# One step of a hybrid decoder on one core: ScalarE weighs the value pages of odd units, VectorE adds them, TensorE keeps those of even units

## What is computed

```
z = q . k / sqrt(128) + bias[h]                    # 8 heads
log_keep = log_sigmoid(-z);  after = sum of log_keep over later keys
a = exp(log_sigmoid(z) + after)
out[h, :] = sum over keys of a[key, h] * v[key, h, :]
```

## Time and profile before

| | us |
|---|---|
| median of 3 runs | 2443.89 |
| lowest, highest run | 2442.11, 2444.17 |
| profiled execution, device time | 2445.29 |
| profiled execution, span | 2443.6 |
| TensorE busy | 2409.5 |
| VectorE busy | 1749.0 |
| ScalarE busy | 1137.6 |
| GpSimd busy | 377.9 |

### The profile page before, as it was taken

How to read it: one execution, slowest core, us unless ns; L and a number is a source line. 1 busy time by engine, 2 the same in 40 slices (tenths; PEclk the granted TensorE clock), 3 DMA queues, 4 the chain that set the end, 5 groups by cost and what they waited for, 6 DMA issues and landing times.

```text
span 2443.6 us, 47247 instructions
## 1 busy us (share of the span) xinstructions
PE 2409.5 (99%) x19728; PEld 2386.2 (98%) x19728; DVE 1749.0 (72%) x2190; ACT 1137.6 (47%) x1719; POOL 377.9 (15%) x375
## 2 busy tenths in 40 slices
PE   8999999999999989999999999999999999999999
PEld 8999999999999989999999999999999999999999
DVE  6379767566665478888888888787888888877333
ACT  6343223334553365555555555555555555555221
POOL 0011111111101320112121212121212121213000
PEclk9999999999999999999999999999999999999999
DMA  6255666464342442566665656565656565685323
GB/s 216 95 193 207 246 238 216 155 211 140 127 173 96 144 161 96 148 147 150 146 153 144 154 144 154 144 155 143 153 144 154 147 150 148 150 190 222 117 87 105
DMA packets 135590, 382.60 MB, mean 157 GB/s; under 512 B 14026, under 2 KB 58186, under 8 KB 126674
## 3 DMA queue, kind: packets, MB, share of 16 engines
q1 hardware_dynamic: 72450, 285.16, 33.9%
q0 software_dynamic: 62640, 94.28, 20.2%
q10 hardware_dynamic: 288, 0.14, 0.0%
HBM read 309.18 MB, written 73.55 MB: 157 GB/s over the span
## 4 chain that ended last, share of the span: by engine, by line
PE 84%; DVE 9%; ACT 2%; issue 2%; DMA 1%; POOL 0%; SPq 0%; ACTq 0%; DVEq 0%; POOLq 0%
PE out_ps L2029 24%; PE tok_mix L2275 15%; PE pair_ps L2275 12%; PE out_ps L2259 9%; PE out_ps L2275 8%; PE out_ps L2348 5%; PE out_ps L2152 3%; PE pair_ps L2348 3%; DVE w_lo L1729 2%; DVE w_sum L1741 2%; PE tok_mix L2348 1%; PE pair_ps L2068 1%; ACT w_hi L1208 1%; DVE w_lo L1734 1%; DMA w_raw<-w_units 1%
## 5 line engine op out<-in xcount | busy, mean ns | idle before, releaser
L2029 PE MATMUL out_ps<-x_hi,w_hi 128*128 128x260 f32 x1792 | 379.1, 293 | 12.1 <-DVE w_lo L1581 7.8
L1208 ACT ACTIVATE w_hi<-w_sum 128x1024 fp32r<-128x1024 f32 (+1 forms) x252 | 215.4, 855 | 341.6 <-DVE w_sum L1741 246.4
L2029 PE MATMUL out_ps<-x_hi,w_lo 128*128 128x260 f32 x1792 | 362.2, 284 | 0.0
L2029 PE MATMUL out_ps<-x_lo,w_hi 128*128 128x260 f32 x1792 | 361.8, 284 | 0.0
L1729 DVE TENSOR_TENSOR w_lo<-w_sum,w_hi 128x1024 fp32r<-128x1024 f32 (+1 forms) x252 | 244.7, 971 | 134.4 <-ACT w_hi L1208 133.8
L1208 ACT ACTIVATE w_hi<-w_raw 128x1024 fp32r<-128x1024 f32 (+1 forms) x306 | 261.2, 865 | 135.5 <-PE out_ps L2259 102.4
L2275 PE MATMUL tok_mix<-op_hi,w_hi 128*128 128x260 f32 x1056 | 297.1, 281 | 1.5 <-ACT part L1250 1.5
L2275 PE MATMUL tok_mix<-op_hi,w_lo 128*128 128x260 f32 x1056 | 298.1, 282 | 0.0
L2275 PE MATMUL tok_mix<-op_lo,w_hi 128*128 128x260 f32 x1056 | 297.5, 282 | 0.0
L2029 PEld LDWEIGHTS out_ps<-x_hi,w_hi 128*128 128x128 f32 x1792 | 279.8, 190 | 15.2 <-DVE w_lo L1581 7.8
L906 POOL DMA_DIRECT2D h_dram<-staging x110 | 146.7, 1485 | 926.5 <-DVE staging L1890 909.2
(11 more groups left out here) (305 smaller groups left out, 6105.9 us busy)
## 6 DMA issues: line engine op xcount, KB each, us to landing
w_raw<-w_units SPq DMA_DIRECT2D x239, 512.0 KB, 4.0
w_raw<-w_units SPq DMA_DIRECT2D x57, 1024.0 KB, 5.4
w_fifth<-w_units SPq DMA_DIRECT2D x58, 512.0 KB, 3.9
h_dram<-staging POOLq DMA_DIRECT2D x110, 260.0 KB, 6.8
k_ring<-cache_k SPq DMA_DIRECT2D x50, 512.0 KB, 5.0
v_ring<-cache_v POOLq DMA_DIRECT2D x38, 512.0 KB, 4.9
h_dram<-part POOLq DMA_DIRECT2D x50, 260.0 KB, 6.7
q_dram<-staging POOLq DMA_DIRECT2D x40, 260.0 KB, 6.4
```

Source lines behind the costliest of these rows:

```text
L1208: act.activation(dst, src, ACT.Copy).then_inc(hi_done, 1)
L2029: mm = pe.matmul(out_ps[:, 2 * (t % 2) + a, 0:HALF], w[:, u % 2, cols], x[:, a * HALF:(a + 1) * HALF], start=first and n == 0, stop=last a ...
```

## The change

A table of pages (`V_PLAN`) says for each by whom it is weighed, in which unit, when it is added and in which slot it lies. Samples 0 to 2 stay with TensorE. From unit 25 to 39 each odd unit has two pages that ScalarE weighs and VectorE adds at the unit's end; even units 26 to 34 have two on TensorE; 36, 38 and 40 have two, two and one that VectorE weighs and adds; unit 41 has one on TensorE. Sample 7 stays with ScalarE, now wholly in places of `o_cm`, weighed in units 41 to 45. In all TensorE has 35 pages in place of 48, ScalarE 24 in place of 8, VectorE 5 in place of 8; it adds 24 times in place of 14, and there are 5 totals in place of 2 (units 28, 32, 36, 41, 45). The total of a sample is the slot of its first page not on TensorE. GpSimd's due times are set anew. The squares of the samples' columns are made in one piece (64 columns) and halved three times, and the last head's squares now count as the first of two steps of `sb_sum_done`; SyncE's wait for one step stays as it is written, TensorE waits for two. `h` tiles 6 to 11 are loaded in unit 41 of SyncE's list.

```diff
@@ -222,53 +222,92 @@
-V_FIRST = [16, 19, 22, 25, 28, 31]
-BY_TENSOR = len(V_FIRST)
-N_TENSOR = BY_TENSOR * PAGES
...
-WEIGH_UNIT = dict(zip(range(SIXTH, N_PAGES), (35, 35, 36, 36, 37, 37, 38, 38) + (39, 39, 41, 41, 42, 43, 43, 44)))
-ADD_UNIT = dict(zip(range(SIXTH, N_PAGES), (35, 35, 36, 36, 37, 37, 38, 38) + (40, 40, 42, 42, 43, 44, 44, 45)))
-V_REDUCE = {39: BY_TENSOR, 45: BY_TENSOR + 1}
-V_SLOT = [j % V_SLOTS for j in range(SIXTH + 1)] + [1 + n % 2 for n in range(PAGES - 1)] + [2, 1, 4, 5, 6, 4, 5, 6]
...
+def v_plan():
+
+    odd = "scalar"
+    plan = [Page("tensor", 16 + 3 * b + pg // 3, None, (PAGES * b + pg) % V_SLOTS) for b in range(3) for pg in range(PAGES)]
+
+    def add(by, slots, weigh, added=None):
+        for slot, u, a in zip(slots, weigh, added or weigh):
+            plan.append(Page(by, u, None if by == "tensor" else a, slot))
+
+    for first, near, far in ((25, 1, 2), (29, 2, 1)):
+        add(odd, (0, near), (first, first))
+        add("tensor", (far, near), (first + 1, first + 1))
+        add(odd, (far, near), (first + 2, first + 2))
+        add("tensor", (far, near), (first + 3, first + 3))
+    add(odd, (0, 1), (33, 33))
+    add("tensor", (2, 1), (34, 34))
+    add(odd, (2, 1), (35, 35))
+    add("vector", (2, 1), (36, 36))
+    add(odd, (2, 1), (37, 37))
+    add("vector", (0, 1), (38, 38))
+    add(odd, (0, 1), (39, 39))
+    add("vector", (0,), (40,))
+    add("tensor", (1,), (41,))
+    add("scalar", (3, 4, 5, 6, 4, 5, 6, 4), (41, 41, 41, 42, 43, 43, 44, 45), (41, 42, 42, 43, 44, 44, 45, 45))
+    return plan
+
+
+V_PLAN = v_plan()
+V_SUM = {28: 3, 32: 4, 36: 5, 41: 6, 45: 7}
+V_UNITS = sorted({(page.weigh, j // PAGES) for j, page in enumerate(V_PLAN) if page.by == "tensor"} | set(V_SUM.items()))
...
+def v_freed(i):
+
+    page = V_PLAN[i]
+    if page.by == "tensor":
+        return page.weigh + (0.9 if i == v_pages(page.weigh)[-1] else 0.7)
+    if is_first(i):
+        return [u for u, b in V_SUM.items() if b == i // PAGES][0] + 0.6
+    late = i + 1 == len(V_PLAN) or V_PLAN[i + 1].add != page.add
+    return page.add + (0.85 if page.add % 2 and page.add < U_OUT else 0.5) + (0.08 if late else 0)
...
@@ -721,11 +757,10 @@
 
                     sp.wait_ge(z_s_done, SAMPLES)
                     sp.dma_start(h[:, 0:H_KEYS, :], x_t[:, 0:H_KEYS, :]).then_inc(h_in[0], 16)
-                if u == U_OUT:
-
-                    sp.wait_ge(v_used, N_TENSOR)
-                    sp.wait_ge(total_used, 1)
-                    sp.wait_ge(v_added, added(SEVENTH + 1))
+                if u == V_UNITS[-2][0]:
+
+                    sp.wait_ge(v_used, pages_by("tensor", N_PAGES - 1))
+                    sp.wait_ge(total_used, len(V_SUM) - 1)
                     sp.dma_start(h[:, H_KEYS:H_PAGES, :], x_t[:, H_KEYS:H_PAGES, :]).then_inc(h_in[1], 16)
                 if u == U_OUT + 4:
@@ -830,18 +865,21 @@
 
             def load_v(j):
                 page = pool.value_load(table[0:1, j:j + 1], min_val=0, max_val=N_PHYS - 1)
-                before = v_before(j)
-                if before is None and V_SLOT[j] >= V_SLOTS:
-                    pool.wait_ge(x_lo_done, KT + HEADS)
-                elif before is not None and before < N_TENSOR:
-                    pool.wait_ge(v_used, before + 1)
-                elif before is not None:
-                    pool.wait_ge(v_added, added(before))
-                elif V_SLOT[j] == RING:
-                    pool.wait_ge(q_rows_out, 16)
+                before, slot_of_v = v_before(j), V_PLAN[j].slot
+                if before is None:
+                    if slot_of_v >= V_SLOTS:
+                        pool.wait_ge(x_lo_done, KT + HEADS)
+                    elif slot_of_v == RING:
+                        pool.wait_ge(q_rows_out, 16)
+                elif V_PLAN[before].by == "tensor":
+                    pool.wait_ge(v_used, pages_by("tensor", before))
+                elif is_first(before):
+                    pool.wait_ge(total_used, sums_before(before // PAGES))
+                else:
+                    pool.wait_ge(v_added, adds_before(before))
                 pool.dma_start(v_slot(j),
                                cache_v[bass.ds(page, 1), :, :].rearrange("a p n -> (a p) n"))\
-                    .then_inc(v_in[V_SLOT[j]], 16)
+                    .then_inc(v_in[V_PLAN[j].slot], 16)
 
             def add_squares(x, total, cols, done=pool_step):
                 chained(pool.tensor_tensor(pool_sq[:, cols], x, x, ALU.mult))
-            freed = [U_OUT - 0.3 if v_before(j) is None else v_freed(v_before(j)) for j in range(V_SLOTS, N_PAGES)]
-            jobs = [(freed[j - V_SLOTS] + 0.8, "load", j) for j in range(V_SLOTS, N_PAGES)]
+            jobs = [(U_OUT + 0.45 if v_before(j) is None else v_freed(v_before(j)), "load", j)
+                    for j in range(V_SLOTS, N_PAGES)]
             jobs += [(U_MLP + 3.5 + 2 * i, "mlp", i) for i in range(HEADS)]
@@ -871,11 +909,16 @@
                     add_squares(o_cm[:, i, :], cm_r, slice(0, TOK), cm_sum_done if i == HEADS - 1 else pool_step)
                 else:
                     pool.wait_ge(tok_read, reads_before("av", U_KV + 3 + 2 * i) + 1)
-                    add_squares(q[:, i, 0:PROMPT], sb_r, slice(0, PROMPT))
+                    add_squares(q[:, i, 0:PROMPT], sb_r, slice(0, PROMPT),
+                                sb_sum_done if i == HEADS - 1 else pool_step)
             pool.wait_ge(v_read, len(V_UNITS))
-            for i in range(HEADS):
-                add_squares(q[:, i, PROMPT:TOK], sb_r, slice(PROMPT, TOK),
-                            sb_sum_done if i == HEADS - 1 else pool_step)
+            samples = q[:, :, PROMPT:TOK]
+            n = HEADS * SAMPLES
+            chained(pool.tensor_tensor(y[:, 0, 0:n].rearrange("p (h s) -> p h s", s=SAMPLES), samples, samples, ALU.mult))
+            while n > SAMPLES:
+                n //= 2
+                chained(pool.tensor_tensor(y[:, 0, 0:n], y[:, 0, 0:n], y[:, 0, n:2 * n], ALU.add))
+            pool.tensor_tensor(sb_r[:, PROMPT:TOK], sb_r[:, PROMPT:TOK], y[:, 0, 0:n], ALU.add).then_inc(sb_sum_done, 1)
...
@@ -1128,13 +1167,15 @@
                     act.wait_ge(out_read, t + 1)
                     square_head(2 * HEADS + i, y[:, t % 2, :])
                     if i:
+                        weigh_pages(u, 0)
                         act.wait_ge(arg_done, i)
                         act.activation(z[:, :], z[:, :], ACT.Exp).then_inc(a_done, 1)
                         weights_of_sample(u)
                     rstd(2 * HEADS + i)
                     if not i:
                         weights_of_sample(u)
-                    weigh_pages(u)
+                        weigh_pages(u, 0)
+                    weigh_pages(u, 1)
                     if i:
                         take_attention(i - 1)
                 elif u <= U_OUT:
...
 
             def add_page(j):
 
-                b, pg = divmod(j, PAGES)
-                if b > BY_TENSOR:
-                    dve.wait_ge(v_scaled, pg + 1)
-                if j == SEVENTH + 1:
-                    dve.wait_ge(x_lo_done, KT + HEADS)
-                total = v_place(V_TOTAL[b])
-                chained(dve.tensor_tensor(total, v_slot(j - 1) if pg == 1 else total, v_slot(j), ALU.add), v_added)
+                if V_PLAN[j].by == "scalar":
+                    dve.wait_ge(v_scaled, pages_by("scalar", j))
+                total = v_slot(v_first(j // PAGES))
+                chained(dve.tensor_tensor(total, total, v_slot(j), ALU.add), v_added)
 
             def pages_of(u):
 
...
 
-                pe.wait_ge(v_added, added(PAGES * b + PAGES - 1))
-                pe.wait_ge(v_read, V_UNITS.index((u, b)))
-                total = v_place(V_TOTAL[b])
+                first = v_first(b)
+                pe.wait_ge(v_added, adds_before(PAGES * (b + 1) - 1))
+                pe.wait_ge(v_read, V_UNITS.index((u, b)) - 1)
                 for hd in range(HEADS):
-                    mm = pe.matmul(o_s_ps(u, b)[:, hd:hd + 1], total[:, hd * P:(hd + 1) * P], ones[:, 0:1],
+                    mm = pe.matmul(o_s_ps(u, b)[:, hd:hd + 1], v_slot(first)[:, hd * P:(hd + 1) * P], ones[:, 0:1],
                                    start=False, stop=True, skip_group_check=True)
-                    between[2] = lambda: sum_features(sb_r, sb_sum_done, 1, (root_done, 3))\
+                    between[2] = lambda: sum_features(sb_r, sb_sum_done, 2, (root_done, 3))\
                         .then_inc(x_sum_ready, 1)
 
                 for at, j in zip((14, 11, 7), reversed(v_pages(u))):
                     between[at] = lambda j=j, u=u: weigh_values(j, u)
-                if u in V_REDUCE:
-                    between[14] = lambda u=u: sum_total(u, V_REDUCE[u])
+                if u in V_SUM:
+                    between[(14, 12, 7)[len(v_pages(u))]] = lambda u=u: sum_total(u, V_SUM[u])
```

More of the change, by code:

```diff
@@ L237 @@
[L237 to L242 removed]
+Page = namedtuple("Page", "by weigh add slot")
+def v_plan():
```

(13 more changed lines are left out.)

66 lines of the change are left out of this document (26 added, 40 removed).

## The result

| | before | after |
|---|---|---|
| median, us | 2444.03 | 2419.64 |
| lowest, highest run (4 runs each) | 2442.11, 2444.60 | 2419.37, 2419.89 |
| profiled execution: device time, span | 2445.29, 2443.6 | 2419.68, 2418.0 |

The ratio is 0.9897, 95% interval 0.9884 to 0.9910: 24.4 us less by the medians, 25.6 us by the two profiled executions. Predicted were 2418.0 us and, against the profiled execution, 25.9 us.

What follows compares the result with a forecast made beforehand. TensorE, busy 2409.5 of 2443.6 us, was taken as the bound. Gains of 17.8 + 2.0 + 6.1 = 25.9 us took 2445.29 to 2419.4, less 1.4 to the median: 2418.0 us, range 2415.0 to 2427.0.

Steps and rivals of the forecast that it cites:

- The sum of the pages, 17.8 us: TensorE, units 25 to 47: 13 pages less, three totals more, net 10 page prices of 1.78 us.
- The 23.8 us of unit 29: Unit 29's length before the change, 460.40 to 484.18; without its three pages of 1.78 us, 18.5 us.
- ScalarE at price 0: Odd units 25 to 39: two pages weighed, 4.9 us a unit, fit into ScalarE's idle times; nothing on the path.
- VectorE at price 0: 8.5 us more VectorE work; an odd unit's two adds fit where it idled 9.94 us; nothing on the path.
- GpSimd's order, 2.0 us: Page loads issued before attention squares; unit 38's pages arrive on time, TensorE's `soft` wait goes: 2.0 us, 0 if late.
- the second rival: Small new waits of 1 to 2 us in four or five places as TensorE's units shorten: 2423 to 2427; chance 0.1.
- The tail, 6.1 us: Units 46 and 47: earlier load of `h` removes TensorE's 3.19 us wait and the half-rate stretch: 6.1 us gained.
- (first): One of the waits in units 46 and 38 stays: 2424.1 or 2420.0 us; chance 0.2.
- (third): Odd units 27 to 39: first page lands late and holds ScalarE's exponential, 6.1 us each: 2460.7 us; chance 0.04.
- The lower end of the range, 2415.0: Whole kernel: the lowest time foreseen, from the highest page price with a wait less.
- The subtraction of 1.4 us: Whole kernel: the profiled execution lay 1.4 us above the runs' median, so 2419.4 was lowered to 2418.0 us.

Runs made afterwards that it cites:

- one_head: Changed kernel, but only the first TensorE page of each unit keeps eight matmuls, the others one of eight (140 matmuls less): 2389.4 us.
- after_both_ahead: Changed kernel with ScalarE weighing both pages of an odd unit ahead of the exponential, none behind the root: 2419.8 us.
- after_vector: Changed kernel with VectorE instead of ScalarE weighing the odd units' pages: 2423.5 us.
- page_34: Changed kernel with head 6's squares of attention one unit later and unit 34's two pages on VectorE instead of TensorE: 2417.8 us.
- before_order: Kernel before, squares of attention due at 3.85 instead of 3.7, so GpSimd issues page loads ahead of them: 2441.7 us.
- the two experiments: Tail edit (samples' squares, release of the h load) made alone in the kernel before: 2440.2 us; then undone in the changed kernel: 2426.6 us.

## Why the prediction was right

- **The sum of the pages, 17.8 us.** Right to 0.1 us in the stages without another term (table above), and one_head confirms the price at 1.80 us. TensorE bounds all units that lost pages. The 23.8 us of unit 29 were read to a row of VectorE; by ScalarE's own row (484.51) they are 24.1, and less three pages 18.8, so that the 18.5 came out a little better than its reading.
- **ScalarE at price 0.** Right, and with more slack than argued: an exponential 0.55 us behind the end of its cover cost nothing (after_both_ahead).
- **VectorE at price 0.** Right, but with a limit that I had not looked for. The step read unit 29 and let it stand for all odd units; unit 39 holds the reciprocal too. Two adds fit there with 1.27 us to spare, with the weighing they do not (after_vector). I had credited ScalarE with nothing by this step; without its weighing the kernel is 2.3 us longer up to unit 48, lost in units 39 and 40 and about half of it by the collision, and 3.9 by the medians. That the adds would have to hold the next tile's read for a whole unit before TensorE noticed was too kind: in page_34 VectorE comes 4.2 us into the unit to `y`, and TensorE waits 0.9 us in that same unit.
- **GpSimd's order, 2.0 us.** Right in the mechanism, late page, late `keep`, late `soft`; neither VectorE nor ScalarE waits for `cache_v` between 380 and 790 us in the changed kernel. The size holds for the execution that it was read from (2.3 by before_order); in another the wait had a slow stretch behind it and cost 4.7 us.
- **What the same move cost.** Not in the prediction: the squares that moved behind the loads now run beside VectorE's splits in unit 40, 0.6 us of wait. It was the kind of loss that the second rival had, but smaller.
- **The tail, 6.1 us.** Measured 5.8 in the profile, 6.0 to 6.4 by the two experiments (7.0 by the medians of the second). The text gave the gain to the early load; either half alone gives it.
- **The rivals.** No large wait stayed (first), the small new waits came to 0.6 us and not 5 to 9 (second), and no page held the exponential (third; its wait is given as 3.3 us, where the earlier trace rows has 3.19). The lower end of the range, 2415.0, lies 2.4 us under what the highest page price alone gives, and the text names no wait that fills this.

The time came out 1.6 us above the forecast by the median, 0.3 us by the profiled executions. That the second is so close is in part luck: the new wait of 0.6 us and the 0.3 us that the tail lacks would leave 25.0, and 0.6 us come back that no edit accounts for. The subtraction of 1.4 us for the profiled execution's distance from the median was the weak step: the distance belonged to the kernel before, whose runs spread, and did not carry over to the changed one, whose profiled execution (2419.68) lies on its median.

## What to carry to other kernels

When one engine bounds, price a move by that engine's own rows (start of the odd work to the start of the next ordinary work) and look at the others for the order of their work in the fullest unit, not in a typical one. A gain on the bound engine ends where another engine's unit is full: there, share the work by kind (one weighs, one adds) rather than by piece. Of a chain of small operations and a load behind it, it is enough to shorten either part below the slack, and a due time that is moved should be checked for what it now runs beside.
